# A sixteen-column bank opener, and one branch's operand halves prepared inside the gate stage

## The reference, cut to what matters

```
xn = rms_norm_2(h, norm_mix_g)
b_c, c_c, h_c, z_s, gate_logits = split(xn @ w_in)
y_conv = (b_c * causal_conv(c_c * h_c)) @ w_up_conv        # 1024 -> 2048
y_sgu  = spatial_gating(z_s) @ w_up_sgu                    # 1024 -> 2048
g_conv, g_sgu = split(sigmoid(gate_logits))
h = h + (g_conv * y_conv + g_sgu * y_sgu) @ w_out
```

## Time and profile before

| what | value |
|---|---|
| median of 3 runs | 2279.1 us (2278.78 to 2279.76) |
| the profiled execution's own time | 2278.47 us |
| span of its trace | 2276.7 us |
| TensorE busy | 2245.7 us of the span (99%) |
| VectorE, ScalarE, GpSimd busy | 71%, 53%, 11% |
| granted TensorE clock, mean | 0.994 |
| line 2437, high products of the feature stages | 638.4 us in 2656 matmuls |
| line 2240, bank openers | 9.7 us in 37 matmuls |

### The profile page before, as it was taken

The page is one execution under the profiler, slowest core; times in us unless marked ns, Lnnn a source line. Parts: engine busy times, 40 slices in busy tenths (PEclk is TensorE's granted clock), DMA queues, the critical chain, the costliest instruction groups (busy, mean ns, idle before and its releaser), DMA issues.

```text
span 2276.7 us, 34661 instructions
## 1 busy us (share of the span) xinstructions
PE 2245.7 (99%) x12090; PEld 1939.1 (85%) x12090; DVE 1605.5 (71%) x1909; ACT 1207.9 (53%) x1229; POOL 252.5 (11%) x108
## 2 busy tenths in 40 slices
PE   9999999999999999999999999999999999999997
PEld 8999788888888888888888888888887888888886
DVE  2999876566555654444586665567458898999997
ACT  4445455444444443434554444444346778787785
POOL 4898201000000000000100000000010000101000
PEclk9999999999999999999999999999989999999999
DMA  7666355676677655555577666655566999999995
GB/s 203 195 173 181 125 189 170 191 192 185 185 191 191 188 184 185 195 192 193 176 199 195 178 185 185 185 169 196 188 222 251 382 369 366 377 370 391 370 374 231
DMA packets 446262, 515.97 MB, mean 227 GB/s; under 512 B 12911, under 2 KB 407831, under 8 KB 410263
## 3 DMA queue, kind: packets, MB, share of 16 engines
q1 hardware_dynamic: 443268, 502.21, 67.6%
q0 software_dynamic: 2656, 12.70, 1.4%
q10 hardware_dynamic: 272, 0.20, 0.0%
HBM read 513.40 MB, written 6.29 MB: 228 GB/s over the span
## 4 chain that ended last, share of the span: by engine, by line
PE 88%; DVE 5%; issue 3%; ACT 2%; DVEq 1%; POOL 0%; ACTq 0%; POOLq 0%
PE ps L2437 25%; PE ps L2331 16%; PE ps L2442 13%; PE ps L2646 10%; PE ps L2663 7%; PE ps L2651 5%; DVE ps L1387 3%; PE ps L2511 2%; ACT whi L728 1%; PE ps L2344 1%; PE ps L2235 1%; PE ps L2236 1%; PE ps L2253 1%; PE ps L2176 1%; PE ps L2383 1%
## 5 line engine op out<-in xcount | busy, mean ns | idle before, releaser
L728 ACT ACTIVATE whi<-raw 128x2048 fp32r<-128x2048 f32 x286 | 547.2, 1914 | 357.2 <-PE ps L2331 183.2
L1307 DVE TENSOR_TENSOR wlo<-raw,whi 128x2048 fp32r<-128x2048 f32 x247 | 565.5, 2290 | 205.2 <-ACT whi L728 205.2
L2437 PE MATMUL ps<-xT,whi 128*128 128x512 f32 x2656 | 638.4, 391 | 5.3 <-DVE xT L1751 4.3
L2437 PEld LDWEIGHTS ps<-xT,whi 128*128 128x128 f32 x2656 | 488.1, 189 | 99.7 <-issue 4.5
L2442 PEld LDWEIGHTS ps<-xT,wlo 128*128 128x128 f32 x2656 | 342.6, 191 | 14.2
L2442 PE MATMUL ps<-xT,wlo 128*128 128x256 f32 x2656 | 347.0, 283 | 0.0
L992 ACT ACTIVATE wk<-ps 128x256 f32<-128x256 f32 x184 | 68.8, 383 | 449.3 <-PE ps L2442 448.9
L2331 PE MATMUL ps<-whi,act 128*128 128x512 f32 x1088 | 257.8, 389 | 0.0
L2331 PEld LDWEIGHTS ps<-whi,act 128*128 128x128 f32 x1088 | 204.1, 188 | 42.7 <-ACT act L910 0.3
L1313 DVE TENSOR_TENSOR wlo<-raw,whi 128x2048 fp32r<-128x2048 f32 x94 | 214.0, 2286 | 3.9 <-ACT whi L738 3.5
L738 ACT ACTIVATE whi<-raw 128x2048 fp32r<-128x2048 f32 x88 | 168.0, 1914 | 31.8 <-PE ps L2646 22.4
(11 more groups left out here) (340 smaller groups left out, 2700.9 us busy)
## 6 DMA issues: line engine op xcount, KB each, us to landing
raw<-in_w_in SPq DMA_DIRECT2D x72, 1024.0 KB, 5.5
raw<-in_w_exp_up SPq DMA_DIRECT2D x56, 1024.0 KB, 7.2
raw<-in_ffn_w_gate SPq DMA_DIRECT2D x44, 1024.0 KB, 5.6
raw<-in_ffn_w_up SPq DMA_DIRECT2D x44, 1024.0 KB, 5.6
raw<-in_ffn_w_down SPq DMA_DIRECT2D x44, 1024.0 KB, 4.7
raw<-in_w_exp_gate SPq DMA_DIRECT2D x40, 1024.0 KB, 6.0
raw<-in_conv_w_in SPq DMA_DIRECT2D x32, 1024.0 KB, 6.0
more_raw<-in_w_exp_down SPq DMA_DIRECT2D x32, 1024.0 KB, 7.7
```

Of the source, the lines that this page charges most:

```text
L728: fn(whi[:, s % 2, :], raw[:, s % RING, :], ACT.Copy).then_inc(hi_ready, 1)
L1307: V.tensor_tensor(wlo[:, s % 2, :], raw[:, s % RING, :], whi[:, s % 2, :], ALU.subtract).then_inc(lo_ready, 1)
L2437: mm(ps[:, bank, :], whi[:, s % 2, at:at + P], xT5[:, k0 + k, :], start=(k == 0), stop=False)
```

## The change

Two edits that have nothing to do with each other.

1. `open_bank` writes 16 columns instead of 512. All 37 calls take the new default. (Line 2321, a product of zeros that is not an opener, stays at 512.)
2. The convolution branch's two halves get a place of their own, `pair`, laid over `tmp`: the high half over the first half of `tmp` (the factor that GpSimd has read by then), the low half over `yc` itself, in place. In each of the eight groups of the gate stage ACT copies one tile (256 columns) behind its second panel, after a wait for all eight of GpSimd's tiles, and DVE subtracts one tile behind its third panel. After the stage only the gating branch's two copies and two subtractions are left, followed by `hi(UP, 1)` and `lo(UP, 1)`. TensorE waits once for all eight tiles of `pair` ahead of UP; the piecewise waits stand at the second panel. The convolution branch's high products read their 512 moving columns as two runs of 256, which lie 2048 elements apart, and write the bank through a view of two times 256.

```diff
+        pair = nc.alloc_sbuf_tensor_at("pair", [P, 2, CT, T], F32R, offset=... start of tmp ...)
 ACT, gt_group(j, m):
                     fn(tile_of(tiles, j, s), xs[:, s % 2, :], ACT.Sigmoid).then_inc(gate_ready, 1)
+                    if s == 1:
+                        a.wait_ge(ys_ready, CT)
+                        fn(pair[:, 0, ds(m, 1), :], yc[:, ds(m, 1), :], ACT.Copy).then_inc(pair_hi, 1)
 ...
             a.wait_ge(mm_done, UP)
-            for q in range(4):
-                src = yc if q < 2 else tiles[:, UT:UT + CT, :]
-                k = (q % 2) * 4
-                if q == 2:
-                    a.wait_ge(ys_ready, CT)
-                fn(xT5[:, 4 * q:4 * q + 4, 0:T], src[:, k:k + 4, :], ACT.Copy).then_inc(pair_hi, 1)
-                if q == 1:
-                    hi(UP, 1)
+            for q in range(2):
+                fn(xT5[:, CT + 4 * q:CT + 4 * q + 4, 0:T], tiles[:, UT + 4 * q:UT + 4 * q + 4, :], ACT.Copy).then_inc(pair_hi, 1)
+            hi(UP, 1)
 DVE, gt_group(j, m):
                     if not (last and s == 3):
                         lo(j + GT, s + 2)
+                    if s == 2:
+                        v.wait_ge(pair_hi, m + 1)
+                        V.tensor_tensor(pair[:, 1, ds(m, 1), :], yc[:, ds(m, 1), :], pair[:, 0, ds(m, 1), :],
+                                        ALU.subtract).then_inc(pair_lo, 1)
 ...
-            for q in range(4):
+            for q in range(2):
...
+            lo(UP, 1)
 TensorE:
-            def open_bank(bank, width=BANK):
+            OPEN_W = 16
+            def open_bank(bank, width=OPEN_W):
...
+                    moving = both(k0 + k)
+                    out_at = ps[:, bank, :] if both is both_halves else ps[:, bank, :].rearrange("p (o c) -> p o c", o=2)
+                    mm(out_at, whi[:, s % 2, at:at + P], moving, start=(k == 0), stop=False)
...
+            pe.wait_ge(pair_lo, CT)
+            up_group(0, arrival=lambda k: pe.wait_ge(pair_lo, CT + (k - CT) // 4 + 1))
```

More of the change, by code:

```diff
@@ L167, in build_program @@
         tH = xT[:, (SLOTS - RING) * PANEL:(SLOTS - RING) * PANEL + TOK * D].rearrange("p (t d) -> p t d", t=TOK)
+        pair = nc.alloc_sbuf_tensor_at("pair", [P, 2, CT, T], F32R, offset=arena_at + 4 * (BIG + (RING + 4) * PANEL + KT * 2 * TM + TOK * D))
         uext = big[:, 0:KT * EXT].rearrange("p (k c) -> p k c", k=KT)
@@ L1076, in _, with gt_group @@
             a.sem_inc(gate_ready, 2)
-            def gt_group(j, last=False):
+            def gt_group(j, m, last=False):
                 for s in range(4):
@@ L1085, in gt_group @@
                     fn(tile_of(tiles, j, s), xs[:, s % 2, :], ACT.Sigmoid).then_inc(gate_ready, 1)
+                    if s == 1:
+                        a.wait_ge(ys_ready, CT)
+                        fn(pair[:, 0, ds(m, 1), :], yc[:, ds(m, 1), :], ACT.Copy).then_inc(pair_hi, 1)
             with a.Fori(0, (2 * KT - 4) // 4) as r:
-                gt_group(r * 4)
-            gt_group(2 * KT - 4, last=True)
+                gt_group(r * 4, r)
+            gt_group(2 * KT - 4, CT - 1, last=True)
             a.wait_ge(mm_done, UP)
-            for q in range(4):
-                src = yc if q < 2 else tiles[:, UT:UT + CT, :]
-                k = (q % 2) * 4
-                if q == 2:
-                    a.wait_ge(ys_ready, CT)
-                fn(xT5[:, 4 * q:4 * q + 4, 0:T], src[:, k:k + 4, :], ACT.Copy).then_inc(pair_hi, 1)
-                if q == 1:
-                    hi(UP, 1)
+            for q in range(2):
+                fn(xT5[:, CT + 4 * q:CT + 4 * q + 4, 0:T], tiles[:, UT + 4 * q:UT + 4 * q + 4, :], ACT.Copy).then_inc(pair_hi, 1)
+            hi(UP, 1)
             def up_group(j):
@@ L1739, in gt_group @@
                         lo(j + GT, s + 2)
+                    if s == 2:
+                        v.wait_ge(pair_hi, m + 1)
+                        V.tensor_tensor(pair[:, 1, ds(m, 1), :], yc[:, ds(m, 1), :], pair[:, 0, ds(m, 1), :],
+                                        ALU.subtract).then_inc(pair_lo, 1)
             with rounds(v, (2 * KT - 4) // 4, (own, 4)) as r:
-                gt_group(r * 4)
-            gt_group(2 * KT - 4, last=True)
+                gt_group(r * 4, r)
+            gt_group(2 * KT - 4, CT - 1, last=True)
             own.wait(v)
-            for q in range(4):
[L1748 to L1751, removed]
+            for q in range(2):
+                k = 4 * q
+                v.wait_ge(pair_hi, CT + q + 1)
+                V.tensor_tensor(xT5[:, CT + k:CT + k + 4, T:2 * T], tiles[:, UT + k:UT + k + 4, :], xT5[:, CT + k:CT + k + 4, 0:T],
                                 ALU.subtract).then_inc(pair_lo, 1)
-                if q == 1:
-                    lo(UP, 1)
+            lo(UP, 1)
             v.wait_ge(gate_ready, 2 * KT + 2)
@@ L2424, in scale_rows, with both_halves, high_half, feature_panel @@
                 i.then_inc(rs_sum, 1)
-            def feature_panel(n, s, f, bank, k0=0, count=KT, part=0, width=P, arrival=None):
+            def both_halves(k):
+                return xT5[:, k, :]
+            def high_half(k):
+                return xT5[:, k, 0:T]
+            def feature_panel(n, s, f, bank, k0=0, count=KT, part=0, width=P, arrival=None, both=both_halves, high=high_half):
                 pe.wait_ge(feat_free, f)
@@ L2436, in feature_panel @@
                         arrival(k0 + k)
-                    mm(ps[:, bank, :], whi[:, s % 2, at:at + P], xT5[:, k0 + k, :], start=(k == 0), stop=False)
+                    moving = both(k0 + k)
+                    out_at = ps[:, bank, :] if both is both_halves else ps[:, bank, :].rearrange("p (o c) -> p o c", o=2)
+                    mm(out_at, whi[:, s % 2, at:at + P], moving, start=(k == 0), stop=False)
                 if part == 0:
@@ L2441, in feature_panel @@
                     at = k * width + part * P
-                    i = mm(ps[:, bank, 0:T], wlo[:, s % 2, at:at + P], xT5[:, k0 + k, 0:T],
+                    i = mm(ps[:, bank, 0:T], wlo[:, s % 2, at:at + P], high(k0 + k),
                            start=False, stop=(k == count - 1))
@@ L2543, in _, with conv_both, conv_high @@
             feature_stage(GT, F_E + GT - CH, 2 * KT)
+            def conv_both(k):
+                return pair[:, :, k, :]
+            def conv_high(k):
+                return pair[:, 0, k, :]
             def up_group(j, arrival=None):
@@ L2549, in up_group @@
                                           k0=(s % 2) * CT, count=CT, part=b, width=2 * P,
-                                          arrival=arrival if s < 2 and b == 0 else None)
+                                          arrival=arrival if s == 1 and b == 0 else None,
+                                          both=both_halves if s % 2 else conv_both, high=high_half if s % 2 else conv_high)
                     i.then_inc(mm_done, 1)
-            up_group(0, arrival=lambda k: pe.wait_ge(pair_lo, k // 4 + 1))
+            pe.wait_ge(pair_lo, CT)
+            up_group(0, arrival=lambda k: pe.wait_ge(pair_lo, CT + (k - CT) // 4 + 1))
             with pe.Fori(1, (2 * CT) // 4) as r:
```

## The result

The changed kernel takes 2267.25 us (median of 5 runs, 2265.97 to 2267.73); the kernel before, run beside it, 2279.31 us (5 runs). The ratio is 0.9948, 95% interval 0.9938 to 0.9959: 12.1 us less, with the interval 9.3 to 14.1 us. The profiled execution took 2265.97 us and its span 2264.2 us.

What follows compares the result with a forecast made beforehand. The prediction took TensorE to bound the kernel (88% of the span). Openers 5.7, restart 3.6 and clock 1.5 us, less 0.1 for the late second panel, give 10.7 us: from 2279.1 to 2268.4 us, range 2266.6 to 2273.4 us.

Steps and rivals of the forecast that it cites:

- Openers: All 37 openers at 16 columns: eight groups of four save 0.66 us each, one 0.39; 5.7 us won, bounds 4.3 to 7.1.
- The group at 1092 us: Opener group followed by products needing DVE's line 1556: at most 0.39 us of 0.96 won before that wait binds.
- Restart: Start of UP: TensorE idles 0.7 us instead of 4.3, waiting for the last new subtraction; 3.6 us won, or 3.0.
- Clock: UP's first eight products run at full clock after the shorter idle stretch: 1.5 us won, 0 if the clock falls anyway.
- Gate stage: Eight ACT copies and eight DVE subtractions inserted there stay hidden from TensorE: cost 0, or 3.6 us if cover were gone.
- UP's second panel: Its `lo` ends near 1508.16, just before TensorE wants `wlo` at 1508.4: cost 0, bound 0.5 us.
- Split operand: The convolution branch's 128 high products, reading two runs of 256, keep their rate: cost 0, at most 1.5 us.
- (a): Rival: openers keep most of their cost, set by load and operand-type change, not columns; 2270.3 to 2274.1 us, chance 0.15.
- (b): Rival: stall moves; clock falls anyway or UP's second panel waits for `wlo`; 1.5 or 0.5 us missing, chance 0.10.
- (c): Rival: the eight insertions in the gate stage reach TensorE, costing 3.6 us; 2272.0 us, chance 0.05.
- (e): Rival: TensorE's wait ahead of UP is met no sooner, the last subtraction being held up on DVE; 2273.4 us, chance 0.05.
- (d): Rival: two-run operand slows UP's even panels to plain fp32 rate, 128 x 0.20 = 25.8 us; 2294.2 us, chance 0.05.

Runs made afterwards that it cites:

- run with the filled gap: The kernel before, with 17 products of ones added between GT and UP into a bank nobody reads: 2276.95 us (10 runs), ratio 0.9991.
- first comparison: The changed kernel with both edits against the kernel before, first measurement: 2267.25 us against 2279.31, ratio 0.9948, 12.1 us less.
- second comparison: The changed kernel, nothing altered, run once more against the kernel before: 2267.73 us (5 runs) against 2278.97, ratio 0.9952, 11.2 us less.

## Why the prediction was right

The mechanisms went as predicted but for one, job 0 of the experts; that the openers' term came out right all the same is luck, since two errors in it cancelled. In the order of its steps:

- **Openers, 5.7 us predicted, 5.7 us in the trace** (5.0 in the run of that part alone, whose profile also lost 1.0 us more at the start of UP). The term was mis-sized where the prediction took "the middle, 0.30 us left, 0.66 us saved": a group saves 0.78 us, since the 4-column products of the earlier trace rows, 112 ns apart, are dearer than openers of 16 columns, 25 ns apart. The eight groups then give 6.2 us, not 5.3. The group at 1092 us gave 0.31 us where 0.39 was the bound, and the single one nothing, both for the waits named in the earlier trace rows. Wrong was "the other eight groups stand in stretches where TensorE follows itself": job 0's group gave 0.70 of its 0.78 us back to a wait for `wlo`, 5 us later, and the other jobs 0.16 us in all. Before, TensorE came to that place just late enough not to wait.
- **Restart, 3.6 us predicted, 3.76 measured.** The wait is for the subtraction that the prediction named, behind the `wlo` it named. TensorE idles 0.51 us where 0.7 was said: `wlo` ended where the prediction has it (1498.41, with everything there 2.0 us ahead of before); the subtraction, which starts before that end (1498.33), adds 0.35 us, not 0.43, and TensorE starts 0.04 us behind it, not 0.13.
- **Clock, 1.5 us predicted, 1.36 measured** at full granted clock; of the prediction's two counts, 1.64 and 1.41, the lower was right. The run with the filled gap shows the cause; the openers-only run shows that the same idle can also cost 2.3 us (1.36 + 0.98).
- **Gate stage, 0 predicted.** Right: the shift grows by 0.02 us across it.
- **UP's second panel, 0 with a bound of 0.5.** Right, closely: its `wlo` starts at 1503.88 and ends 2.29 us later, at 1506.17; its low products start at 1506.34.
- **Split operand, 0 with a bound of 1.5.** Right: 1.84 us for eight products in both kinds of half-panel.

The rivals: (a) fell, since 0.19 of 0.96 us are left of a group; (b), (c) and (e) have no place in the trace; (d) fell with the half-panels (its 128 x 0.20 us are 25.6 us, not 25.8, which decides nothing). The steps of the trace add up to 10.8 us where the prediction has 10.7. The 1.4 us by which the first comparison went past that sum have the size of the shorter router stage in the profiled execution, which no step of the prediction spoke of; the second comparison, 11.2 us, came closer.

## What to carry to other kernels

An idle stretch of the bounding engine can cost more than its length, so operands that are ready early belong in the stage before, where ACT and DVE have gaps, even if only tile by tile. A small saving on the bounding engine is kept only until the next place where another engine is nearly late: compare the shifts stage by stage, not the sum. And before an opener is made cheaper, ask whether the first real product can carry its flag: here that won a further 0.38 us per group of four, half as much as narrowing it did, in the trace; the times alone do not tell it from nothing.

## What the runs showed of the hardware

- One-row bf16 products start 216, 56, 26 and 25 ns apart at 512, 128, 56 and 16 columns: from 56 to 16 columns the spacing no longer falls. Their weight loads of 91 ns run beside each other.
- A start flag on a product of 16 columns opens the whole bank: the products behind it write all 512 columns with `start=False`, and the sums are those of the kernel with openers of 512.
- Four such openers between fp32r products cost 0.38 us, of which the openers' spacings make about 0.09 us.
- After the same 4.3 us idle, the low clock cost UP's first half-panel 1.36 us in one execution and 2.3 us in another.
- An operand read as two runs of 256 columns, 2048 elements apart, costs what one run of 512 does: 1.84 us for eight products.
